# Seven block products in place of eight for the first gate chunk of the last branch

## The reference: a decoder layer with four gated mixers and an FFN

```
h = rms_norm(x)
z = h @ w_in                       # columns: inputs of four mixers, then four gates of 1024 columns each
o_n = mixer_n(z)                   # sparse attention, pooling, gated MLP, stick-breaking attention; 256 wide each
proj_n = o_n @ w_branch[n]         # 256 -> 1024
merged = sum_n sigmoid(gate_n) * proj_n
x = x + merged @ w_out
x = x + (silu(rms_norm(x) @ w_gate) * (rms_norm(x) @ w_up)) @ w_down
```

## Time and profile before

| | |
|---|---|
| time, median of 3 runs | 755.65 us (755.02 to 755.95) |
| time of the profiled execution | 754.7 us, 1.8 us more than its span |
| span of the profile | 752.9 us, TensorE clock granted 0.999 |
| TensorE busy | 747.9 us (99%) |
| VectorE busy | 592.7 us (79%) |
| ScalarE busy | 404.8 us (54%) |
| GpSimd busy | 104.9 us (14%) |

### The profile page before, as it was taken

One profiled execution on the slowest core, in us unless ns is written; L12 is line 12 of the kernel. 1 busy time (PEld: TensorE's weight loads), 2 busy tenths in 40 slices (PEclk: granted clock), 3 DMA queues, 4 the chain that ended last, 5 costly groups with the idle time before them and its releaser, 6 DMA issues.

```text
span 752.9 us, 11500 instructions
## 1 busy us (share of the span) xinstructions
PE 747.9 (99%) x4506; PEld 660.9 (88%) x4506; DVE 592.7 (79%) x819; ACT 404.8 (54%) x629; POOL 104.9 (14%) x131
## 2 busy tenths in 40 slices
PE   8999999999999999999999999999999999999998
PEld 8988888888888888788888899999889999999887
DVE  6655988878788976425978989889989888888991
ACT  6654545456663665445349656556544556666430
POOL 6200050457203221211231000000000000000000
PEclk9999999999999999999999999999999999999999
DMA  8371113221133122317226625335073333338102
GB/s 292 96 239 56 57 58 112 82 87 57 57 111 112 57 93 75 112 57 279 85 93 169 185 113 167 114 111 199 5 260 110 109 110 109 113 113 328 66 26 84
DMA packets 67877, 89.55 MB, mean 119 GB/s; under 512 B 3108, under 2 KB 52592, under 8 KB 67696
## 3 DMA queue, kind: packets, MB, share of 16 engines
q1 hardware_dynamic: 66224, 85.60, 34.0%
q0 software_dynamic: 1456, 3.09, 2.0%
q10 hardware_dynamic: 144, 0.13, 0.1%
HBM read 81.99 MB, written 4.19 MB: 114 GB/s over the span
## 4 chain that ended last, share of the span: by engine, by line
PE 99%; DVE 0%; issue 0%; POOL 0%; ACT 0%; POOLq 0%; DVEq 0%
PE bank L2365 15%; PE bank L2367 15%; PE bank L2366 15%; PE bank L2795 8%; PE bank L2794 8%; PE bank L2793 8%; PE bank L2874 5%; PE bank L2876 5%; PE bank L2878 5%; PE bank L2732 2%; PE bank L2733 2%; PE bank L2734 2%; PE bank L2764 1%; PE bank L2765 1%; PE bank L2763 1%; PE bank L2580 1%
## 5 line engine op out<-in xcount | busy, mean ns | idle before, releaser
L2365 PE MATMUL bank<-h_hi,w_hi 128*128 128x512 f32 (+1 forms) x352 | 134.7, 383 | 0.0
L2367 PE MATMUL bank<-h_hi,w_lo 128*128 128x512 f32 (+1 forms) x352 | 133.7, 380 | 0.0
L2366 PE MATMUL bank<-h_lo,w_hi 128*128 128x512 f32 (+1 forms) x352 | 133.6, 379 | 0.0
L2793 PE MATMUL bank<-t_hi,w_hi 128*128 128x256 f32 x320 | 88.4, 276 | 0.0
L2795 PE MATMUL bank<-t_hi,w_lo 128*128 128x256 f32 x320 | 88.3, 276 | 0.0
L2794 PE MATMUL bank<-t_lo,w_hi 128*128 128x256 f32 x320 | 88.3, 276 | 0.0
L1538 DVE TENSOR_TENSOR w_lo<-raw,w_hi 128x2048 fp32r<-128x2048 f32 x27 | 64.2, 2381 | 23.4 <-ACT w_hi L927 16.1
L2367 PEld LDWEIGHTS bank<-h_hi,w_lo 128*128 128x128 f32 x352 | 66.2, 188 | 12.7
L2365 PEld LDWEIGHTS bank<-h_hi,w_hi 128*128 128x128 f32 x352 | 66.2, 188 | 12.6 <-issue 0.3
L2366 PEld LDWEIGHTS bank<-h_lo,w_hi 128*128 128x128 f32 x352 | 66.2, 188 | 12.1
L2794 PE MATMUL bank<-f_lo,w_hi 128*128 128x256 f32 x240 | 66.3, 276 | 0.0
(11 more groups left out here) (382 smaller groups left out, 1862.6 us busy)
## 6 DMA issues: line engine op xcount, KB each, us to landing
raw<-in_w_in_dram SPq DMA_DIRECT2D x26, 1024.0 KB, 5.0
raw<-in_w_ffn_up_dram SPq DMA_DIRECT2D x11, 1024.0 KB, 4.9
raw<-in_w_ffn_gate_dram SPq DMA_DIRECT2D x10, 1024.0 KB, 5.0
raw<-in_w_ffn_down_dram SPq DMA_DIRECT2D x7, 1024.0 KB, 5.0
raw<-in_w_branch_dram SPq DMA_DIRECT2D x4, 1024.0 KB, 4.7
b<-in_w_ffn_down_dram SPq DMA_DIRECT2D x4, 1024.0 KB, 6.7
x_sb<-in_x_dram SPq DMA_DIRECT2D x6, 512.0 KB, 4.6
o<-in_w_out_dram SPq DMA_DIRECT2D x3, 1024.0 KB, 9.2
```

What stands on the lines that cost most here:

```text
L2365: mm(dst, l_hi, r_hi, start=start, stop=False)
L2366: mm(dst, l_hi, r_lo, start=False, stop=False)
L2367: return mm(dst, l_lo, r_hi, start=False, stop=stop)
L2793: mm(dst, l_hi, r_hi, start=begin and k == 0, stop=False, skip_group_check=True)
```

## The change: chunk 27 as seven block products

Chunk 27 (`SEVEN`), the first gate chunk of the last branch, becomes an eighth kind of chunk that goes through `wino_chunk`. Its two tiles are no longer made one after the other in `bank[0]` and `bank[1]`, but together in banks 6, 7, 2 and 3, and its tile 1 is taken before its tile 0 (`gate_tiles`). New work prepares it:

- GpSimd adds the high and low parts of four blocks of `h` back together (`whole_block`, eight additions of 128x512), between its additions to `merged` in chunk 24.
- VectorE forms four sums of these blocks (`gate_sums`), four sums of weight blocks (`weight_sums`), and the low parts of both (`gate_lows`, `weight_lows`); ScalarE makes the high parts.
- While the seven products run, ScalarE and VectorE carry the partial results (`seven_products`).

The work for the output weights changes places: `o22` is loaded right after chunk 27's weights, `o11` and `o12` share one semaphore, and `out_behind` starts two tiles later, with `o11`'s low part after tile 3 in place of tile 0, and `OT1`'s after the last tile.

```diff
+    SEVEN = MIXER_CHUNKS - D // CW
+    assert chunks[SEVEN][4] == ("gate", N_BRANCH - 1, 0)
+    chunks[SEVEN] = ("seven",) + chunks[SEVEN][1:]
+    def gate_tiles(c):
+        return (1, 0) if c == SEVEN else (0, 1)
...
+        SEVEN_BANK = (bank[6], bank[7], bank[2], bank[3])
...
@@ SP @@
                     sp.wait_ge(filled, fill_at[PROJ_AT[N_BRANCH - 1] + 1])
                     load_out(o11[:, :], 0, 0, "o11_in")
-                    load_out(o12[:, :], 0, 1, "right_half_in")
+                    load_out(o12[:, :], 0, 1, "o11_in")
+                load(c)
+                if c == SEVEN:
+                    sp.wait_ge(filled, fill_at[PROJ_AT[N_BRANCH - 2] + 1])
                     load_out(o22[:, :], 1, 1, "right_half_in")
-                load(c)
...
@@ GpSimd @@
+                    if (m, d) == (N_BRANCH - 2, 4):
+                        pool.wait_ge(S["prob_turned"], HEADS * TT)
+                        whole_block(g_sum[:, T1], LOWER, T2ND)
+                        whole_block(g_sum[:, T2], UPPER, T2ND)
+                    elif (m, d) == (N_BRANCH - 2, 5):
+                        whole_block(g_first, LOWER, T1ST)
+                        whole_block(g_sum[:, T4], UPPER, T1ST)
                     pool.wait_ge(S["gated"], y + 1)
...
@@ ScalarE: branch_tiles, evac, seven_products @@
-                    if d in halves_at:
+                    if c + 1 == SEVEN:
+                        if d < 4:
+                            wino_split(SEVEN, (0, 2, 3, 1)[d])
+                    elif d in halves_at:
                         split_half(c + 1, d == halves_at[1])
...
+                    if j == 1 and c == SEVEN - 2:
+                        for n, i in enumerate((2, 0, 1, 3)):
+                            act.wait_ge(S["t_made"], SEVEN_SUMS - 3 + n)
+                            nact.activation(g_hi[:, i], g_sum[:, i], ACT.Copy).then_inc(S["t_hi_ready"], 1)
...
+            def seven_products():
+                f0, f1, first, last = SEVEN_BANK
+                act.wait_ge(S["product_done"], 1)
+                nact.activation(f0[:, T1ST], first[:, T1ST], ACT.Copy).then_inc(S["c11_seeded"], 1)
+                act.wait_ge(S["product_done"], 2)
+                nact.activation(gate_seventh[:, :], last[:, T1ST], ACT.Copy).then_inc(S["seventh_copied"], 1)
...
@@ VectorE: seven_products, the loop over chunks @@
+            def seven_products():
+                _, f1, first, _ = SEVEN_BANK
+                dve.wait_ge(S["product_done"], 3)
+                dve.wait_ge(S["seventh_copied"], 1)
+                vec.tensor_tensor(f1[:, T1ST], first[:, T1ST], gate_seventh[:, :], ALU.add).then_inc(S["c21_seeded"], 1)
+                dve.wait_ge(S["product_done"], 6)
+                dve.wait_ge(S["c12_seeded"], 1)
+                vec.tensor_tensor(f1[:, T2ND], first[:, T1ST], gate_seventh[:, :], ALU.add).then_inc(S["c22_ready"], 1)
+                dve.wait_ge(S["o11_in"], 16 * 2)
+                out_difference(o12[:, :], o12[:, :], o11[:, :], 0)
...
@@ VectorE: out_behind @@
                 elif d == 6:
+                    first_sums(slice(0, 2))
+                elif d == 7:
                     dve.wait_ge(lo_ready, MIXER_CHUNKS)
                     out_low(OT1)
-                    first_sums(slice(0, 2))
...
+                if c == SEVEN - 2:
+                    gate_sums()
...
+                if c == SEVEN - 3:
+                    weight_sums(SEVEN, (0,))
+                elif c == SEVEN - 2:
+                    weight_lows(SEVEN, 0)
+                    gate_lows(1, 4)
+                    for step in (2, 3, 1):
+                        weight_lows(SEVEN, step)
                 slot(c)
+                if c == SEVEN - 3:
+                    weight_sums(SEVEN, (1,))
...
@@ TensorE: the loop over chunks @@
+                if c == SEVEN:
+                    wino_chunk(c)
+                    continue
```

More of the change, by code:

```diff
@@ L176, in hybrid_layer @@
         chunks[c] = ("plain",) + chunks[c][1:]
-    WINO = [c for c in range(NC) if chunks[c][0] == "ffn"]
+    WINO = [SEVEN] + [c for c in range(NC) if chunks[c][0] == "ffn"]
+    FIRST_WINO = WINO[1]
+    SEVEN_SUMS = 8
     wino_index = {c: m for m, c in enumerate(WINO)}
@@ L1051, in branch_tiles @@
                     nact.activation(branch[:, d, :], bank[f % 2][:, :], ACT.Copy).then_inc(taken[f % 2], 1)
-            OUT_BEHIND = {("gate", N_BRANCH - 1, q): u for q, u in ((0, O11), (2, O21), (3, OT1))}
+            OUT_BEHIND = {("gate", N_BRANCH - 1, q): u for q, u in ((1, O11), (2, O21))}
             def evac(c):
@@ L1264, in _ @@
                 if chunks[c][4] == ("gate", N_BRANCH - 1, D // CW - 1):
+                    out_high(OT1)
                     merged_high(KT - 1)
@@ new lines, in gate_sums @@
+            def gate_sums():
+                T1, T2, T3, T4 = (g_sum[:, i] for i in range(4))
+                made = SEVEN_SUMS - 4
+                dve.wait_ge(S["t_made"], made)
+                vec.tensor_tensor(T3, T2, T1, ALU.subtract).then_inc(S["t_made"], 1)
+                dve.wait_ge(S["t_made"], made + 1)
+                vec.tensor_tensor(T1, T1, g_first[:, :, :], ALU.subtract).then_inc(S["t_made"], 1)
+                dve.wait_ge(S["t_made"], made + 2)
+                vec.tensor_tensor(T2, T2, T1, ALU.subtract).then_inc(S["t_made"], 1)
+                dve.wait_ge(S["t_made"], made + 3)
+                vec.tensor_tensor(T4, T4, T2, ALU.subtract).then_inc(S["t_made"], 1)
@@ new lines, in gate_lows @@
+            def gate_lows(first, end):
+                for n, i in tuple(enumerate((2, 0, 1, 3)))[first:end]:
+                    dve.wait_ge(S["t_hi_ready"], n + 1)
+                    vec.tensor_tensor(g_lo[:, i], g_sum[:, i], g_hi[:, i].bitcast(F32), ALU.subtract)\
+                        .then_inc(S["t_lo_ready"], 1)
+            def seven_products():
[8 more added lines that the diff above has]
+                out_difference(o12[:, :], o12[:, :], o11[:, :], 0)
@@ L1903, in gated @@
             def gated(c):
                 _, m, q = chunks[c][4]
-                for j in range(CT):
+                for n, j in enumerate(gate_tiles(c)):
                     d = CT * q + j
-                    y = (m - 1) * KT + d
+                    y = (m - 1) * KT + CT * q + n
                     if q == 0:
                         wait_taken(dve, fill_at[PROJ_AT[m]] + d)
-                    wait_taken(dve, fill_at[c] + j)
+                    if c == SEVEN:
+                        dve.wait_ge(S["gate_taken"], n + 1)
+                    else:
+                        wait_taken(dve, fill_at[c] + j)
```

338 lines of the change are left out of this document (198 added, 140 removed).

## The result

The changed kernel takes 757.71 us (median of 7 runs, 757.31 to 758.81), the kernel before 755.27 (median of 7, 754.99 to 755.95) beside it: 2.44 us more, a ratio of 1.0031 with a 95% interval of 1.0019 to 1.0043. The change made the kernel slower, by 0.3%; the prediction was 758.2, with 757 to 760 for its likeliest case. The profiled execution took 757.32 us, with a span of 755.6.

The account below looks back on a forecast made before the run. TensorE, busy for 99% of the span, was taken to bound the kernel. -1.36 + 1.2 + 1.25 + 1.45 + 0.4 gave +2.9 to +3.0 us, forecast 758.2 us, range 753.9 to 760.6.

Parts of the forecast that it names:

- TensorE's work: Chunk 27: 84 matmuls of 128x256 replace 48 of 128x512 on TensorE, a gain of 1.36 us.
- rival (e): Chunk 27: the 36 more weight loads are not hidden, +2.7 us, 757.4 to 758.4, no TensorE wait; chance 0.02.
- Step 1: Preparing the blocks, chunks 24 to 26: TensorE waits 0.5 us at the second projection tile; chunk 29 loads about 344.1.
- a third wait: A trace of 0.04 us among three TensorE waits up to chunk 27, place not given, plus 0.15 for restarting.
- Step 2: Inside chunk 27's seven products: TensorE's third product waits 0.2 us for ScalarE's first carry.
- A restart's price: Wherever TensorE has stopped, beginning again with a weight load costs 0 to 0.4 us, taken as 0.15.
- Step 3: Transfers: `o12`, queued behind chunk 29's weights, lands at 355.3, so VectorE stands for 2.5 us (0 to 4).
- Step 4: VectorE's backlog from `o12` on: TensorE waits 1.1 us at chunk 30, 1.3 at the last `mg_lo` tile, 0.25 next unit.
- The sum: Whole kernel: -1.36 + 1.2 + 1.25 + 1.45 + 0.4 = +2.9 to +3.0 us.
- (b): Transfers in time, `o12` there at 353: chunk 30's wait vanishes, the last tile's shrinks to 0.4; +0.8 us; chance 0.25.
- (c): GpSimd's additions meet no long VectorE operation, so only the first carry costs TensorE; -1.0 us, 753.7 to 754.7; chance 0.12.
- (d): Chunk 29's load later by more, or the queue slower: 1.5 us more, 759.2 to 761; chance 0.08.
- (a): VectorE's backlog reaches TensorE as summed, by +1.5 to +4.5 us; chance 0.53.

Follow-up runs that it names:

- experiment 1: Changed kernel with `o11` and `o12` loaded ahead of chunk 29's weights; +0.12 us against the kernel before, ratio 1.0001.
- experiment 2: Changed kernel with GpSimd's eight additions of the last branch cut to 8 of 512 columns each; -0.34 us against the kernel before, ratio 0.9996.
- experiment 3: Changed kernel with two block-sum roundings put behind chunk 25's second tile and early carries ahead of chunk 28's split; +2.07 us against the kernel before.
- experiment 10: Changed kernel with the tail, carry and front edits of 5, but chunk 29 again loaded ahead of `o11` and `o12`; +1.50 us against the kernel before.
- 4: Changed kernel with `OT1`'s low part behind that of sum S2 and `O22`'s behind S1's; +1.10 us against the kernel before, ratio 1.0013.
- experiment 9: Changed kernel with `o11` and `o12` ahead of chunk 29 and `OT1`'s low part behind S2's, chunks 24 to 27 unchanged; -0.22 us against the kernel before.
- 5: Changed kernel with `o11`, `o12` ahead of chunk 29, `OT1`'s low part behind S2's, early carries and reordered front roundings; -1.60 us against the kernel before.
- 11: Kernel of 5 with VectorE instead of GpSimd making the eight last additions; 754.38 us, -1.07 us against the kernel before, ratio 0.9988.

## Why the prediction was right, step by step

**TensorE's work**, -1.36: right. 0.1133 per matmul in the last 48 of chunk 27. The rule of the Trainium skill that was weighed against it ("TensorE: Matmul & The Clock Gate", section "Back-to-back issue gap") would have put 98 ns there by the estimate made from it, and 131 where the trace has 227; here it misses, and rival (e) with it.

**Step 1**: right to a tenth. With the 0.50 off, chunk 26's split starts at 324.9 (predicted 324.8), ScalarE's second tile of chunk 25 ends at 333.7 (333.6 to 333.7), VectorE's last low part ends at 344.1 (344.0), and chunk 29's load goes out at 344.1 (344.1). The stop of TensorE was 0.62, where 0.5 and a restart of 0.15 were predicted. Of the sum for steps 1 and 2 (1.2 predicted, 1.14 measured) one part is luck: a third wait in it, 0.19 with its restart, whose place the prediction doesn't give, is not in the trace, and the slower steps of 0.17 in all, which nobody foresaw, stand in for it. ScalarE's row, with the start of that tile and the first carry behind the split of chunk 28:

```profile
333.62 0.58 ACT L1198 ACTIVATE two<-bank 128x512 f32<-128x512 f32 x1
...
344.89 1.91 ACT L979 ACTIVATE w_hi<-raw 128x2048 fp32r<-128x2048 f32 x1
346.70 0.38 ACT L1209 ACTIVATE bank<-bank 128x256 f32<-128x256 f32 x1
```

**Step 2**: 0.2 and a restart of 0.15 predicted, 0.36 measured.

**A restart's price**, 0.15: measured 0.16 to 0.18. At chunk 30 TensorE was due at 375.89 (375.66 and a step), the split was there at 376.26: 0.37 of waiting, 0.55 lost. At the last tile it was due at 394.85, the tile there at 396.05: 1.20 and 1.36. (The 0.4 us that the prediction took for a bound is no wait in the middle: in the trace of the kernel before it stands at 10.21, among the first matmuls.)

**Step 3**: the mechanism was right, the size too large. `o12` landed at 355.0, with the 0.50 off 354.5, where I had 355.3. I had taken the 11.2 us from chunk 29's issue to `o12`'s landing from the kernel before, where `o12` was issued two microseconds behind chunk 29; here they are one apart, and it was 10.4.

**Step 4**: from the start of `o12`'s difference to the end of chunk 30's split 21.23 us (predicted 21.0), from there to the last `mg_lo` 19.8 (20.2; the prediction's 396.3 is a slip, 376.3 and 20.2 make 396.5). Four meetings ahead of chunk 30 and four behind it, as counted. Because the row began 0.8 us earlier than predicted and took 0.2 longer, and TensorE came 0.2 later than predicted (the slower steps of the projection), the stop at chunk 30 was 0.55 instead of 1.25. Of the waits this is the one that was mis-sized; that at the last tile (1.36 against 1.45) and at the next unit (0.39 against 0.4) stood, since there TensorE and the tile both came about 0.6 to 0.8 sooner than predicted.

**The sum**: 1.2 + 1.25 + 1.45 + 0.4 = 4.3 predicted, 3.44 measured; +3.0 predicted for the time, +2.44 measured. The prediction put at nothing the steps less than 0.04 too long (0.34) and what comes behind the last matmul (-0.29); that it lost nothing by this is luck.

**The rivals.** (b) would have needed `o12` at 353: experiment 1 made it so and found the tail's stop at 0.41, as (b) had it (0.4), and about no change (+0.12, where (b) had +0.8). (c) had additions that meet nothing: eight meetings stood in the trace, and experiment 2, which takes them away, gives its price (-0.34 instead of the -1.0 of (c), as the stops of the front and of the carry stay). (d) had chunk 29's load or the queue late by more: the load went out as forecast, and `o12` landed sooner. (The chances of (a), (d) and (e) make 0.63 by themselves, not the 0.62 of the prediction's last sum; nothing hangs on it.) One thing must not be read into the sum. It is an account of lost steps, and as that it held; it does not say what taking one stop away would win. VectorE's row starts from a transfer and not from TensorE, so a stop of the front only shortens the one at chunk 30: experiment 3 moved TensorE's arrival there by 0.5 us and the time by less than can be told, and in experiment 10, beside 4, the front's stops went and the time did not fall. The 1.2 us of steps 1 and 2 were real stops, but while `o12` is late, taking them away wins nothing that can be told.

## What to carry to other kernels

Where a second engine is busy for 96% of a stretch, work out its row from the last thing that it waits for, and count each meeting with a third engine as a part of it; here that row, not the stops ahead of it, set when TensorE could go on. Stops of the bounding engine can be won one by one only when nothing else paces it: take away the pacing one first (here the place of one load in its queue, worth 2.3 us), then the others are worth what they show (the front's 1.1 us: 1.4 from experiment 9 to 5, nothing from 4 to 10). A change that takes work from the bounding engine may be right and still lose, and its list of waits then tells what order the rest needs: reordered, the same seven products were 1.1 to 1.6 us faster than the kernel before.

## What the runs showed of the hardware

- The list of waits understates a stop of TensorE: 1.10, 0.35, 0.31 and 0.16 us listed were 1.36, 0.62, 0.55 and 0.39 us lost, and the stop of 0.36 at the first carry is not listed. A matmul of 512 columns shows 0.39 us where the next is due after 0.2267, and the step behind a stop is 0.08 to 0.11 longer.
- Behind the stop at the second projection tile two or three single steps of that stage are 0.27 to 0.30 us instead of 0.2267, in each run that has the stop and in none without it (5, 10, 11). Why is open.
- Three transfers of 1 MB issued within about a microsecond: by the fifth experiment's landing times the second came 7.3 us after its issue, and the third when ScalarE had waited for it, 9.3 us after its own. Which of them is late is decided by the order in which they are issued.
- A meeting with an addition costs a VectorE operation 0.91 to 1.10 us, at 512, 2048 and (for two `mg_lo` tiles, 1.86 against 0.76) 256 elements. It goes by what is left of the addition and not by the operation's size: 1.22 us left made `O11`'s low part 1.09 longer, 1.04 left made `OT1`'s 0.91 longer (3.20 against 2.29).
